# Chunk stage of a recurrent layer: new order of its fill and of SyncE's transfers, values turned by transposes, products of constants left out

## The reference

```python
    def step(S, inp):
        r_t, w_t, k_t, v_t, a_t, b_t = inp
        sa = jnp.einsum('bhij,bhj->bhi', S, a_t)
        S = (S * w_t[:, :, None, :] + sa[..., None] * b_t[:, :, None, :]
             + v_t[..., None] * k_t[:, :, None, :])
        return S, jnp.einsum('bhij,bhj->bhi', S, r_t)
    seq_in = tuple(u.transpose(1, 0, 2, 3) for u in (r_h, w_h, k_h, v_h, -kk, kk * a_h))
    _, y = lax.scan(step, S0, seq_in)
```

## Time and profile before

| | us |
|---|---|
| median of 3 runs | 1512.23 (1511.02 to 1512.6) |
| the profiled execution | 1514.68 |
| its span | 1513.0 |
| TensorE busy | 1436.7 (95%) |
| VectorE busy | 1033.1 (68%) |
| ScalarE busy | 739.6 (49%) |
| GpSimd busy | 93.5 (6%) |
| mean granted TensorE clock | 0.981 of full |

### The profile page before, as it was taken

The page is one execution under the profiler, slowest core; times in us unless marked ns, Lnnn a source line. Parts: engine busy times, 40 slices in busy tenths (PEclk is TensorE's granted clock), DMA queues, the critical chain, the costliest instruction groups (busy, mean ns, idle before and its releaser), DMA issues.

```text
span 1513.0 us, 30344 instructions
## 1 busy us (share of the span) xinstructions
PE 1436.7 (95%) x12931; PEld 1322.3 (87%) x12931; DVE 1033.1 (68%) x1463; ACT 739.6 (49%) x1071; POOL 93.5 (6%) x120
## 2 busy tenths in 40 slices
PE   6999999999999999998999967999799999999997
PEld 5898898999999999998999756889467898899986
DVE  5667577588844787577868665776678884488732
ACT  4555465445532455457588532433454553255422
POOL 3010011000030000000000231110000000000010
PEclk9999999999999999999999977999999999999999
DMA  4212221423433333555222232332333343334331
GB/s 126 67 57 63 64 70 50 113 84 98 123 92 100 92 92 88 158 162 173 83 74 77 70 85 47 60 57 40 113 84 98 98 123 104 95 85 112 86 96 56
DMA packets 283990, 136.78 MB, mean 90 GB/s; under 512 B 65449, under 2 KB 278593, under 8 KB 283601
## 3 DMA queue, kind: packets, MB, share of 16 engines
q1 hardware_dynamic: 283552, 134.77, 32.4%
q10 hardware_dynamic: 304, 0.08, 0.0%
HBM read 124.33 MB, written 10.49 MB: 89 GB/s over the span
## 4 chain that ended last, share of the span: by engine, by line
PE 74%; DVE 11%; ACT 6%; issue 3%; DMA 3%; POOL 1%; SPq 0%; DVEq 0%; POOLq 0%; ACTq 0%
PE psg L1882 25%; PE psx L1723 13%; PE psg L1723 11%; PE psg L2688 6%; PE psg L590 2%; DVE w_lo L136 2%; PE psx L590 2%; PE psg L618 2%; PE psg L674 1%; ACT rest_hi L330 1%; PE psx L3334 1%; DVE rest_lo L429 1%; DVE sum_lo L446 1%; ACT rest L316 1%; ACT w_hi L132 1%
## 5 line engine op out<-in xcount | busy, mean ns | idle before, releaser
L132 ACT ACTIVATE w_hi<-w_raw 128x1024 fp32r<-128x1024 f32 (+1 forms) x122 | 141.9, 1164 | 209.8 <-PE psg L1882 148.1
L1882 PE MATMUL psg<-mid_hi_l,w_hi 128*128 128x264 f32 (+1 forms) x720 | 232.8, 323 | 2.3 <-DVE w_lo L136 1.3
L1882 PE MATMUL psg<-mid_lo_l,w_hi 128*128 128x264 f32 (+1 forms) x720 | 231.6, 322 | 0.0
L1882 PE MATMUL psg<-mid_hi_l,w_lo 128*128 128x264 f32 (+1 forms) x720 | 231.0, 321 | 0.0
L136 DVE TENSOR_TENSOR w_lo<-w_raw,w_hi 128x1024 fp32r<-128x1024 f32 (+1 forms) x121 | 165.0, 1365 | 77.5 <-ACT w_hi L132 77.0
L1882 PEld LDWEIGHTS psg<-mid_hi_l,w_hi 128*128 128x128 f32 x720 | 135.3, 188 | 14.1 <-DVE w_lo L136 2.0
L1882 PEld LDWEIGHTS psg<-mid_lo_l,w_hi 128*128 128x128 f32 x720 | 135.3, 188 | 10.5 <-issue 0.2
L1882 PEld LDWEIGHTS psg<-mid_hi_l,w_lo 128*128 128x128 f32 x720 | 135.4, 188 | 10.3
L2688 PE MATMUL psg<-x_hi,w_hi 128*128 128x264 f32 (+1 forms) x320 | 99.7, 312 | 7.9 <-DVE w_lo L136 7.9
L2688 PE MATMUL psg<-x_lo,w_hi 128*128 128x264 f32 (+1 forms) x320 | 98.8, 309 | 0.0
L2688 PE MATMUL psg<-x_hi,w_lo 128*128 128x264 f32 (+1 forms) x320 | 98.7, 309 | 0.0
(11 more groups left out here) (518 smaller groups left out, 4336.1 us busy)
## 6 DMA issues: line engine op xcount, KB each, us to landing
w_raw<-in_w_ffn_out_dram SPq DMA_DIRECT2D x40, 704.0 KB, 4.7
w_raw<-in_w_qkv_dram SPq DMA_DIRECT2D x24, 512.0 KB, 3.7
w_raw<-in_w_rkv_dram SPq DMA_DIRECT2D x24, 512.0 KB, 3.9
x_raw_l<-in_w_ffn_in_dram SPq DMA_DIRECT2D x18, 512.0 KB, 4.1
x_raw_l<-in_w_ffn_in_dram SPq DMA_DIRECT2D x36, 256.0 KB, 4.7
w_raw<-in_w_ffn_in_dram SPq DMA_DIRECT2D x16, 512.0 KB, 3.8
y_raw_l<-in_w_ffn_in_dram SPq DMA_DIRECT2D x16, 512.0 KB, 4.0
y_raw_l<-in_w_ffn_in_dram SPq DMA_DIRECT2D x32, 256.0 KB, 4.5
```

The lines of the kernel that those rows point to most:

```text
L132: k.nc.scalar.activation(k.w_hi[j][:, 0:kt, :], k.raw[j][:, 0:kt, :], ACT.Copy).then_inc(k.hi_ready[j].h, 1)
L1882: done = k.nc.tensor.matmul(self.bank(i, c), w[:, t, :], x, start=t == 0 and n == 0, stop=t == count - 1 and n == 2)
```

## The change

SyncE: `low_kept` becomes two buffers. The low products of chunks 0 and 1 go out and come back first, around the transfers of zeros; then the loop runs over n with keep_inverse(n), fetch_inverse(n), keep_low(n+1), fetch_lanes(n+1), where the last two stood first. TensorE: the fill is written out (chunk 0's turning, quads and a_v stand between l_products(1) and l_products(2)), l_products(3) and the gate of chunk 0 move within step 0, `keep` goes, and `turn_v` uses transposes in place of products with the identity. For that, values lie in partitions 0 to 63 and u in 64 to 127 (akm, uv and chain_u follow), and keys take place 0 of bk and the aa rows place 1. VectorE, ScalarE and GpSimd get fills of their own; wt of chunk 0 and the state update of step 0 move forward, the rounding split of g2 behind wt, and `center` behind the products of chunk 2 on GpSimd. Steps 1 to 8 keep their order on TensorE, VectorE and ScalarE. The core of the diff:

```diff
-    k.low_kept, k.inv_kept, k.turned_kept = (nc.dram_tensor(n, [H, (C // W) * LANE], F32).ap()
-                                             for n in ("low_kept", "inverse_kept", "inverse_turned_kept"))
+    kept = lambda name: nc.dram_tensor(name, [H, (C // W) * LANE], F32).ap()
+    k.low_kept = [kept(f"low_kept{q}") for q in range(2)]
+    k.inv_kept, k.turned_kept = kept("inverse_kept"), kept("inverse_turned_kept")
...
-            for c in range(-3, CHUNKS):
-                step(c, c + 1, c % 2, 0 <= c, 0 <= c + 1 < CHUNKS)
+            for c in range(CHUNKS):
+                step(c, c + 1, c % 2, c + 1 < CHUNKS)
...
         def sync(sp):
             def keep_low(n):
                 sp.wait_ge(low_r.h, n + 1)
-                if n:
-                    sp.wait_ge(lane_in.h, 16 * n)
+                if n >= 2:
+                    sp.wait_ge(lane_in.h, 16 * (n - 1))
                 for half in range(2):
-                    sp.dma_start(by_heads(k.low_kept, half), low[n % 3][half_rows(half), :, :]).then_inc(low_out.h, 16)
+                    sp.dma_start(by_heads(k.low_kept[n % 2], half), low[n % 3][half_rows(half), :, :]).then_inc(low_out.h, 16)
 
             def fetch_lanes(n):
                 sp.wait_ge(low_out.h, 32 * (n + 1))
                 if n >= 2:
                     sp.wait_ge(inv_r.h, 2 * (n - 2) + 1)
-                sp.dma_start(square(lane_low[n % 2]), by_lanes(k.low_kept)).then_inc(lane_in.h, 16)
+                sp.dma_start(square(lane_low[n % 2]), by_lanes(k.low_kept[n % 2])).then_inc(lane_in.h, 16)
...
+            keep_low(0)
+            sp.wait_ge(zero_r.h, 1)
             rest = (C // W) * LANE * H // P - KT * C
             for t in (k.inv_kept, k.turned_kept):
                 flat_t = t.rearrange("h f -> (h f)").rearrange("(p f) -> p f", p=P)
                 zeros = xt[0][:].rearrange("p m c -> p (m c)")
                 sp.dma_start(flat_t[:, 0:KT * C], zeros).then_inc(inv_in.h, 16)
                 sp.dma_start(flat_t[:, KT * C:KT * C + rest], zeros[:, 0:rest]).then_inc(inv_in.h, 16)
-            for c in range(-3, CHUNKS - 2):
-                if c + 3 < CHUNKS:
-                    keep_low(c + 3)
-                    fetch_lanes(c + 3)
-                if c == -3:
-                    sp.wait_ge(scaled_v.h, 1)
-                    sp.dma_start(r.g_raw[:, 0, :, :], g2.src(0, 0)).then_inc(g_in.h, 16)
-                    for at in range(0, P, G_REST):
-                        sp.dma_start(r.g_raw[at:at + G_REST, 1, :, :], g2.src(0, 1)).then_inc(g_in.h, 16)
-                    sp.wait_ge(inv_in.h, 64)
-                else:
-                    keep_inverse(c + 2)
-                    fetch_inverse(c + 2)
+            fetch_lanes(0)
+            keep_low(1)
+            fetch_lanes(1)
+            sp.wait_ge(scaled_v.h, 1)
+            sp.dma_start(r.g_raw[:, 0, :, :], g2.src(0, 0)).then_inc(g_in.h, 16)
+            for at in range(0, P, G_REST):
+                sp.dma_start(r.g_raw[at:at + G_REST, 1, :, :], g2.src(0, 1)).then_inc(g_in.h, 16)
+            sp.wait_ge(inv_in.h, 64)
+            for n in range(CHUNKS):
+                keep_inverse(n)
+                fetch_inverse(n)
+                if 1 <= n < CHUNKS - 1:
+                    keep_low(n + 1)
+                    fetch_lanes(n + 1)
...
+            def lower(n):
+                act.wait_ge(lps.h, n + 1)
+                nc.scalar.activation(low[n % 3][:], l_ps, ACT.Copy).then_inc(low_r.h, 1)
...
+            def values_turned(n, p):
+                act.wait_ge(tv_d.h, n + 1)
+                nc.scalar.activation(uv[p][0:C, :, :].rearrange("p (two m) c -> p m two c", two=2),
+                                     pair_ps[0:C].rearrange("p b (m two c) -> p (b m) two c", two=2, c=C), ACT.Copy)\
+                    .then_inc(uvv_r.h, 1)
...
-                if c + 3 < CHUNKS:
-                    act.wait_ge(lps.h, c + 4)
-                    nc.scalar.activation(low[c % 3][:], l_ps, ACT.Copy).then_inc(low_r.h, 1)
+                if c + 3 < CHUNKS and c:
+                    lower(c + 3)
                 if prep:
-                    act.wait_ge(tb_d.h, n + 1)
-                    nc.scalar.activation(bkt[p][:].rearrange("p m a c -> p (m a) c"),
-                                         pair_ps.rearrange("p b (m c) -> p (b m) c", c=C),
-                                         ACT.Copy).then_inc(bkt_r.h, 1)
-                if 1 < c + 4 < CHUNKS:
+                    keys_turned(n, p)
...
+                if c == 0:
+                    lower(3)
...
+                if c == 0:
+                    gate_out(0)
...
             decays(1)
+            lower(0)
+            keys_turned(0, 0)
+            decays(2)
+            lower(1)
+            values_turned(0, 0)
+            end_decay(0, 0)
+            av_out(0, 0)
+            act.wait_ge(g_in.h, (1 + P // G_REST) * 16)
+            nc.scalar.activation(r.g_hi[:], r.g_raw[:], ACT.Copy).then_inc(g_split.h, 1)
+            decays(3)
+            lower(2)
             steps(act, step)
 
...
-            nc.gpsimd.tensor_scalar(r.center, k.heads[:], -1.0 / HD, None, ALU.mult).then_inc(zero_r.h, 1)
-            pool.wait_ge(zero_r.h, 1)
-            nc.gpsimd.tensor_tensor(r.center, r.center, k.ident[:], ALU.add).then_inc(zero_r.h, 1)
             pool.wait_ge(scaled_v.h, 1)
             front_evicted(pool)
-            nc.gpsimd.memset(turned, 0.0).then_inc(zero_r.h, 1)
             nc.gpsimd.memset(xt[0][:], 0.0).then_inc(zero_r.h, 1)
+            products(1)
             nc.gpsimd.memset(lane_x[:], 0.0).then_inc(zero_r.h, 1)
-            nc.gpsimd.memset(ch.state[:], 0.0).then_inc(zero_r.h, 1)
-            pool.wait_ge(zero_r.h, 6)
+            pool.wait_ge(zero_r.h, 2)
             nc.gpsimd.memset(lane_x[:, 0:W * (W + 1)].rearrange("l (i s) -> l i s", s=W + 1)[:, :, 0:1], 1.0)\
                 .then_inc(zero_r.h, 1)
-            for n in range(1, CHUNKS):
+            nc.gpsimd.memset(ch.state[:], 0.0).then_inc(zero_r.h, 1)
+            nc.gpsimd.memset(turned, 0.0).then_inc(zero_r.h, 1)
+            products(2)
+            nc.gpsimd.tensor_scalar(r.center, k.heads[:], -1.0 / HD, None, ALU.mult).then_inc(zero_r.h, 1)
+            pool.wait_ge(zero_r.h, 6)
+            nc.gpsimd.tensor_tensor(r.center, r.center, k.ident[:], ALU.add).then_inc(zero_r.h, 1)
+            for n in range(3, CHUNKS):
                 products(n)
 
...
+            def step(c, n, q, prep):
                 p = 1 - q
-                if c == 0:
+                dve.wait_ge(av_r.h, c + 1)
+                if c:
+                    dve.wait_ge(w_d.h, c)
+                    nc.vector.scalar_tensor_tensor(wt[:], wy_ps, -1.0, av[q][:], ALU.mult, ALU.subtract)\
+                        .then_inc(wt_r.h, 1)
+                else:
+                    nc.vector.tensor_scalar(wt[:], av[q][:], -1.0, None, ALU.mult).then_inc(wt_r.h, 1)
                     dve.wait_ge(g_split.h, 1)
                     nc.vector.tensor_tensor(r.g_lo[:], r.g_raw[:, 0], r.g_hi[:, 0].bitcast(F32), ALU.subtract)
                     nc.vector.tensor_tensor(r.g_hi[C:P, 1], r.g_raw[C:P, 1], r.g_hi[C:P, 1].bitcast(F32),
                                             ALU.subtract).then_inc(g_split.h, 1)
-                if chain:
-
-                    dve.wait_ge(av_r.h, c + 1)
-                    if c:
-                        dve.wait_ge(w_d.h, c)
-                        nc.vector.scalar_tensor_tensor(wt[:], wy_ps, -1.0, av[q][:], ALU.mult, ALU.subtract)\
-                            .then_inc(wt_r.h, 1)
-                    else:
-                        nc.vector.tensor_scalar(wt[:], av[q][:], -1.0, None, ALU.mult).then_inc(wt_r.h, 1)
-                    if not prep:
-                        for j in range(2):
-                            unit_lo(k, dve, u0 + j, KT)
-                if prep and n:
+                    grow(q, c)
+                if not prep:
+                    for j in range(2):
+                        unit_lo(k, dve, u0 + j, KT)
+                if prep:
                     next_t(n)
-                if 0 <= c + 2 < CHUNKS:
+                if c + 2 < CHUNKS:
                     last_blocks(c + 2)
-                if prep and n:
+                if prep:
                     next_xt(n, p, 0)
                     next_xs(n, p)
-                if chain and prep:
-                    dve.wait_ge(s_d.h, c + 1)
-                    nc.vector.tensor_tensor(ch.state[:], ch.state[:], s_ps, ALU.add).then_inc(s_step.h, 1)
-                    dve.wait_ge(s_step.h, c + 1)
-                    dve.wait_ge(wend_r.h, c + 1)
-                    nc.vector.tensor_tensor(ch.state[:], ch.state[:], w_end[q][:].broadcast_to([P, KT, C]),
-                                            ALU.mult).then_inc(state_r.h, 1)
+                if prep and c:
+                    grow(q, c)
                 if prep:
                     keys(n, 0)
                     reads(n, p, 0)
                     keys(n, 1)
```

(117 more changed lines are left out.)

47 lines of the change are left out of this document (22 added, 25 removed).

## The result

The changed kernel takes 1540.74 us (1538.92 to 1541.49) against 1512.41 (1511.02 to 1513.68): ratio 1.0186, 95% interval 1.0168 to 1.0203, so 28.3 us slower. Forecast were 1533.4 us and a range of 1519 to 1547.

A forecast was written before the change was run, and what follows sets the result against it. The chunk stage was bound by a chain over TensorE and VectorE, without transfers. Fill +5.8, four periods +11.8, a fifth +5.3, last steps -1.7 make +21.2 us; from the median 1512.23 that gives 1533.4 us, range 1519 to 1547.

The forecast's parts named there:

- Part 2: SyncE's new order makes lanes land late in the chunk stage: +11.8 us over four periods, +5.3 for W(5) to W(6).
- The ring: Closed loop of waits over VectorE and SyncE, one turn per step: 20.9 us between wt starts, ends 19.1 and 22.4.
- W: W(c) is the start of wt on VectorE in step c; the count of each period begins there.
- Part 1: turn_v on TensorE by eight transposes: 1.02 us, saving 0.87 a step, 6.1 us over steps 1 to 7 if today's chain remains.
- Part 3: Rewritten fill at the start of the chunk stage: W(1) at 952.5 against 946.73, +5.8 us, bounds +2 and +9.
- Steps 6 and 7: Last steps, without lanes, keep the transposes' gain: 2 x 0.87 = 1.7 us.
- Behind the stage: After the last gate nothing is shielded, the residual's load included: a delay of that gate delays the end.
- Rival A: SyncE's new order finds lanes landed in time, the ring does not bind: -4.2 us, 1508.0 us; chance 0.06.
- rival B: Lanes in time but W(1) another 4 us later at half clock, or a ring at 17.5: 1510 to 1515; chance 0.02.
- rival E: Transposes in turn_v take as long as the products they replace: 1.7 us later, 1535; shares the forecast's 0.76.
- Rival C: The ring binds and pauses before chain_u drop TensorE's clock each step: half the periods at 25 us, 1543; chance 0.14.
- Rival D: TensorE at half clock to the end of the stage, five periods of 25 us: some 1570 us; chance 0.02.

The follow-up runs named there:

- e1: Changed kernel with SyncE's old order restored (keep_low and fetch_lanes ahead of keep_inverse and fetch_inverse): 1501.72 us, ratio 0.9929 to the kernel before.
- e3: Kernel before with only the new SyncE order and two low_kept buffers; fill, products of constants and turning as before: 1533.07 us, ratio 1.0139.
- e2: Kernel before with only values turned by eight transposes and the rows flipped; orders and products of constants as before: 1505.81 us, ratio 0.9952.
- e8: The changed kernel measured and traced once more, nothing edited: 1540.29 us, ratio 1.0182 to the kernel before.
- e10: e1 measured once more, the same kernel in a second turn: 1502.32 us, ratio 0.9928 to the kernel before.
- e4: Changed kernel with 28 unread products of constants ahead of chain_u in steps 1 to 6: 1536.76 us, ratio 1.0158 to the kernel before.

## Why the prediction was right

- **Part 2, the order on SyncE: right.** It decides. e1 and e3 show it from both sides. The ring was forecast at 20.9 us and is 21.3 in the mean. Its terms: W to the second write 5.2 (forecast 5.24). Write to fetch 3.93, 3.94, 3.96, 4.26, 2.62, mean 3.7 (forecast 3.1): this one was too small. The four fetches 2.63 in three turns, 3.40 and 3.22 in two, mean 2.9 (forecast 2.65). keep_low to fetch_lanes 4.14, 4.39, 3.99, 3.32, 3.31, mean 3.8 (forecast 4.5): too large, the single row at 901.89 was above the mean of that place. Lanes asked for to read 2.9 (forecast 2.6), small_blocks 2.6. That the sum is off by only 0.4 us is partly luck: errors of 0.6 and 0.7 us have opposite signs.
- **Part 1, the transposes: right, a little small.** Eight take 1.0 us, and e2 gives 7 us where 6.1 on the path (7 in the expectation of e2) were forecast. That the change of partitions does nothing was wrong by 0.2 us a step.
- **Part 3, the fill: right in its sign, 2 us short.** chain_u(0) was forecast at 922.4 and ran at 925.30. The term that was mis-sized is the first, up to small_blocks(0), and most of it is the clock. TensorE and VectorE in the fill of the changed kernel:

```profile
883.47 1.91 PE L3369 MATMUL psx<-ident,rows 128*64 128x128 f32 x8
886.49 1.97 PE L3384 MATMUL psx<-rows,bk 64*128 64x64 f32 x16 [1.11 <-ACT uv L3065]
...
925.30 1.66 PE L3456 MATMUL psx<-wt,xt 64*64 64x64 f32 x26 [19.42 <-DVE wt L3288]
```

```profile
891.88 0.16 DVE L3211 TENSOR_SCALAR lane_x<-lane_low 64x8 f32<-64x8 f32 x1
...
922.11 0.17 DVE L3211 TENSOR_SCALAR lane_x<-lane_low 64x8 f32<-64x8 f32 x1 [10.78 <-DMA lane_low<-low_kept]
```

  The turning of values at 883.47 took 1.91 and quads 1.97 us: TensorE had paused for 2.4 us before l_products(1), and from 883 on the clock was at the half level. I had these blocks at full clock (1.0 and 1.2). small_blocks(0) thus starts at 891.88 instead of 889.3, 14.3 us behind the start of the stage where 11.2 were counted. e1 runs the same program up to there with the same pause, but its clock stayed full to 887: turning 1.06, quads 1.11 and 1.26, and small_blocks(0) after 11.6 us. e8 has 13.5. So behind the same pause the clock fell at 883 in one execution and at 887 in the other. From small_blocks(0) to small_blocks(2) the count held (30.2 us, forecast 29.9), and from there to chain_u (3.2). From chain_u to W(1) it was 28.8 us, forecast 30.1, which takes back a part of the miss. e1 shows that the new fill is good without the ring: it takes 4 us less than e2, which has the old fill and the products of constants (ratios 0.9929 and 0.9928 against 0.9952; the intervals just overlap). In the traces that difference lies ahead of W(1): 62.7 and 63.9 us from the start of the stage in e1 and e10, 67.4 in e2.
- **Steps 6 and 7: wrong.** Forecast was a gain of 1.7 us, measured a loss of 1.0 in this trace and a gain of 0.5 in e8's. W(6) to W(7) is 14.58 here (forecast 14.8), but in step 7 times_x waits 1.6 us for the fetch of the inverse of chunk 8, the last transfer behind the ring (fetches at 1070.11 to 1073.21), and behind this pause the clock is at the half level from 1077 to 1081. In e8 that wait is 0.3 us and the clock stays full, but chain_u of step 6 runs at half clock behind the ring's last pause. The step that failed is that I let the ring end with the last lanes: its last turn also delivers an inverse, and its last pause can still cost clock.
- **Behind the stage: right.** The delay behind the last gate reaches the end but for about 1 us: the load of the residual is 28.0 us later, the span 26.8 us longer.
- **Rival A** (lanes in time) fell with the first row of VectorE's waits, **rival B** with the time, **rival E** with eight records of turn_v in 1.06 us. **Rival C**: the clock does drop in the pauses, as between 974 and 985, but it recovers within the period, and the ring does not contain it: from wt to the second write of the inverse it is 5.20 us behind W(1) at full clock and 5.19 behind W(2) at half. e3 at full clock (20.4 us) and e4 with filled pauses (21.1) have nearly the same ring. **Rival D** and the rule of the Trainium skill ("TensorE: Matmul & The Clock Gate", Part 4: PE-mode transpose), by which the full clock does not engage for transposes: e2 has sixteen transposes in each step and a granted clock of 1.00 from 944 to 1016; transposes among matmuls do not cost the full clock here. Whether a long run of transposes alone would is not shown.

One reading of the first page was off: the two slices with a clock under 0.9 lie at 870 to 946 us, not near 900 to 970. Nothing in the sum used it.

What stays open: why the write of the inverse took near 3.9 us to its fetch in most turns and 2.6 in others, when the clock falls behind a pause, and which part of the 4 us between e1 and e2 comes from which move in the fill.

## What to carry to other kernels

On a queue that works in order, a transfer costs the place it stands in: put the one whose data are ready first and whose reader comes first ahead, and price a move by the loop that it closes (data ready, waits of all issues ahead, landing, reader, next data), not by its own time. A queue that isn't in the chain of waits today is cover, and a reordering can use up all of it: here 17 us of period had a ring of 21 put beside it. A second buffer did not help here against a wait in program order. Products that only keep the clock up gave 0.9 us by the medians, which is inside the intervals, and a half clock seen beside a loss can be its consequence. And compare a term with a second trace of the same kernel before you explain it: the start of small_blocks(0) differs by 2.1 us between e1 and e10, which are one kernel.

## What the runs showed that I had not expected

The masks akm and arm on VectorE follow 0.61 us behind the instruction before them, instead of 0.72 and 0.71, when akm works in partitions 0 to 63 (e1 and e2 against the first kernel and e3). And a version faster than both kernels came out of undoing one thing: e1, with the new fill, the transposes, no products of constants and the old order of transfers, takes 1501.7 us, 0.9929 (0.9912 to 0.9946) of the kernel before.
